# A hybrid decoder block: second and third gate matrices both by seven block products

## The reference, cut to what matters

```
h = rms_norm(x, norm_mix_pre)
a_h, a_b, a_c, c_a, c_g, s_u, s_v, g_a, g_c, g_s = split(h @ w_in)      # ten 1024-wide parts
y_a = a_b * conv3(a_c * a_h)
y_c = silu(layer_norm(conv31(c_a * sigmoid(c_g)) + b))
y_s = gelu(s_u) * (W_s @ layer_norm(gelu(s_v)) + b_s)
merged = sigmoid(g_a) * (y_a @ w_branch[0]) + sigmoid(g_c) * (y_c @ w_branch[1])
       + sigmoid(g_s) * (y_s @ w_branch[2])
x = x + rms_norm(merged @ w_out, norm_mix_post)          # then a squared-ReLU MLP, 1024 -> 4096 -> 1024
```

## Time and profile before

| | |
|---|---|
| time, median of 3 runs | 949.27 us (949.09 to 950.10) |
| the profiled execution's own time | 950.25 us |
| its span, first to last instruction | 948.5 us |
| mean granted TensorE clock | 0.998 |
| PE busy | 938.9 us (99%) |
| DVE busy | 738.4 us (78%) |
| ACT busy | 444.8 us (47%) |
| POOL busy | 110.0 us (12%) |
| DRAM traffic over the span | 241 GB/s |

### The profile page before, as it was taken

One profiled execution on the slowest core, in us unless ns is written; L12 is line 12 of the kernel. 1 busy time (PEld: TensorE's weight loads), 2 busy tenths in 40 slices (PEclk: granted clock), 3 DMA queues, 4 the chain that ended last, 5 costly groups with the idle time before them and its releaser, 6 DMA issues.

```text
span 948.5 us, 13659 instructions
## 1 busy us (share of the span) xinstructions
PE 938.9 (99%) x4967; PEld 811.5 (86%) x4967; DVE 738.4 (78%) x865; ACT 444.8 (47%) x548; POOL 110.0 (12%) x145
## 2 busy tenths in 40 slices
PE   8999999999999999999999999999999999999997
PEld 7888888888888888888889988899889989989985
DVE  5578978878878988886589575589875875786698
ACT  6533333333333322224368443377745745754774
POOL 1211101001100002222210000121001001100101
PEclk9999999999999999999999999999999999999999
DMA  8467779678776844444597674438586765858763
GB/s 308 152 208 245 233 216 271 187 233 247 196 226 213 218 133 133 133 133 134 149 262 237 217 221 135 178 137 242 155 259 128 236 176 148 232 135 242 197 203 111
DMA packets 45503, 185.36 MB, mean 195 GB/s; under 512 B 5305, under 2 KB 7745, under 8 KB 42177
## 3 DMA queue, kind: packets, MB, share of 16 engines
q1 hardware_dynamic: 32880, 115.52, 34.4%
q0 software_dynamic: 8432, 44.57, 24.2%
q10 hardware_dynamic: 4144, 24.65, 7.0%
HBM read 178.42 MB, written 49.81 MB: 241 GB/s over the span
## 4 chain that ended last, share of the span: by engine, by line
PE 97%; DVE 1%; DMA 1%; issue 0%; ACT 0%; ACTq 0%; DVEq 0%
PE ps L1944 25%; PE ps L1948 25%; PE ps L1946 25%; PE ps L2174 6%; PE ps L2176 6%; PE ps L2178 6%; PE ps L2139 1%; PE ps L2143 1%; PE ps L2141 1%; PE ps L2026 1%; DMA glu<-xt_in 1%; PE ps L2083 1%; PE ps L1989 0%; DVE wide L1782 0%; DVE wide L1799 0%
## 5 line engine op out<-in xcount | busy, mean ns | idle before, releaser
L853 ACT ACTIVATE w_hi<-raw 128x1024 fp32r<-128x1024 f32 (+1 forms) x140 | 146.0, 1052 | 233.7 <-DMA raw<-units_in 122.1
L1340 DVE TENSOR_TENSOR w_lo<-raw,w_hi 128x1024 fp32r<-128x1024 f32 (+1 forms) x141 | 172.0, 1226 | 72.0 <-ACT w_hi L853 68.8
L1429 DVE SCALAR_TENSOR_TENSOR conf<-glu,cols,conf (+1 forms) x240 | 186.8, 778 | 27.5 <-DVE conf L1429 26.4
L1944 PE MATMUL ps<-a_hi,w_hi 128*128 128x512 f32 x512 | 200.0, 391 | 0.0
L1948 PE MATMUL ps<-a_hi,w_lo 128*128 128x512 f32 x512 | 199.3, 389 | 0.0
L1946 PE MATMUL ps<-a_lo,w_hi 128*128 128x512 f32 x512 | 199.2, 389 | 0.0
L1948 PEld LDWEIGHTS ps<-a_hi,w_lo 128*128 128x128 f32 x512 | 96.1, 188 | 20.1
L1946 PEld LDWEIGHTS ps<-a_lo,w_hi 128*128 128x128 f32 x512 | 96.2, 188 | 19.7
L1944 PEld LDWEIGHTS ps<-a_hi,w_hi 128*128 128x128 f32 x512 | 96.1, 188 | 19.7
L1944 PE MATMUL ps<-w_hi,h_hi 128*128 128x512 f32 x220 | 85.8, 390 | 0.1
L1946 PE MATMUL ps<-w_lo,h_hi 128*128 128x512 f32 x220 | 85.6, 389 | 0.0
(11 more groups left out here) (225 smaller groups left out, 1785.8 us busy)
## 6 DMA issues: line engine op xcount, KB each, us to landing
raw<-units_in SPq DMA_DIRECT2D x123, 512.0 KB, 4.2
weight_sums<-units_in POOLq DMA_DIRECT2D x18, 1024.0 KB, 8.4
raw<-weight_sums SPq DMA_DIRECT2D x20, 512.0 KB, 4.3
raw_v<-units_in SPq DMA_DIRECT2D x18, 512.0 KB, 6.6
glu<-units_in SPq DMA_DIRECT2D x16, 512.0 KB, 8.2
glu<-units_in POOLq DMA_DIRECT2D x16, 512.0 KB, 5.5
raw_d<-units_in POOLq DMA_DIRECT2D x15, 512.0 KB, 6.7
glu<-weight_sums SPq DMA_DIRECT2D x9, 512.0 KB, 5.6
```

Of the source, the lines that this page charges most:

```text
L853: return nc.scalar.activation(dst, src, ACT.Copy, scale=scale)
L1340: return nc.vector.tensor_tensor(dst, src, hi, ALU.subtract)
L1429: nc.vector.scalar_tensor_tensor(out=conf[:, tile, :], in0=glu[:, tile, k:k + SEQ], scalar=cols[:, tile, COL_CONF + k:COL_CONF + k + 1], i ...
L1944: nc.tensor.matmul(ps[:, bank, :], left_hi, right_hi, start=first, stop=False, skip_group_check=on_top)
```

## The change

g_s is taken out of the pairs and done by seven block products as g_c is; the differences of x are made once and serve both matrices. The order becomes: w_branch[2] on y_s alone by eight channel units (`U_BS`, units 72 to 79), its result copied by ACT from PSUM into `bs_home`; then 28 gate units (`U_G`, 80 to 107): products 1, 2, 4 of g_s (80 to 85), 1, 2, 4 of g_c (86 to 91), 5, 3, 6, 7 of g_s (92 to 99), 5, 3, 6, 7 of g_c (100 to 107); then w_branch[1] (108 to 115). The layer norm of y_c now runs under units 72 to 79 and the first gate units. `statistic(0)` stands behind unit 75, `statistic(1)` behind unit 78. The sum of squares moves from POOL to DVE. POOL issues eight more DMAs of 1 MB for the block sums of the second matrix, two for each made product. DVE multiplies gate and branch of g_s in four blocks (`gate_s`) into `merged`. The split of y_c moves to between products 6 and 7 of g_c. The reload of x for the residual moves into the w_branch[1] stage, in two parts. Core of the diff:

```diff
-U_G = U_GATE + 4 * KT
-G_UNITS = 14
+U_BS = U_GATE + 2 * KT
+U_G = U_BS + KT
+G_UNITS = 28
 U_B = U_G + G_UNITS
...
-G_MADE = (5, 7, 6, 4)
+G_MADE = (5, 6, 4, 7)
 G_SUMS = MATRICES * MADE_UNITS
 G_FIRST = {5: (0, 0), 7: (1, 1), 6: (1, 1), 4: (1, 0)}
 G_SECOND = {5: (0, 1), 7: (0, 1)}
 G_SOURCE = {6: 5, 4: 6}
-G_ORDER = (1, 2, 4, 5, 3, 6, 7)
-G_BANK = {1: 0, 6: 0, 7: 0, 2: 4, 4: 6, 5: 2, 3: 2}
+G_ORDER = ([(m, product) for m in (GATE_S, GATE_C) for product in (1, 2, 4)] +
+           [(m, product) for m in (GATE_S, GATE_C) for product in (5, 3, 6, 7)])
+G_BANK = ({1: 0, 6: 0, 7: 0, 2: 2, 4: 4, 5: 2, 3: 2}, {1: 6, 6: 6, 7: 6, 2: 2, 4: 4, 5: 4, 3: 4})
 G_ON_TOP = (6, 7, 3)
...
-        g_home = nrm
-        g_of = {name: g_home[:, CH * n:CH * (n + 1), HALF_T * t:HALF_T * (t + 1)]
-                for name, (t, n) in {"22": (0, 0), "21": (0, 1), "11": (1, 1), "12": (1, 0)}.items()}
+        g_home = over("g_home_s", [P, KT, SEQ], "b_lo"), conf
+        bs_home = over("bs_home", [P, KT, SEQ], "b_hi")
+        def g_blocks(home):
+            return {name: home[:, CH * n:CH * (n + 1), HALF_T * t:HALF_T * (t + 1)]
+                    for name, (t, n) in {"22": (0, 0), "21": (0, 1), "11": (1, 1), "12": (1, 0)}.items()}
+        g_of = g_blocks(g_home[GATE_S]), g_blocks(g_home[GATE_C])
+        bs_of, merged_of = g_blocks(bs_home), g_blocks(merged)
...
-                    g_sum(G_MADE[(j - 1) // 2], (j - 1) % 2)
+                    g_sum(GATE_S, G_MADE[(j - 1) // 2], (j - 1) % 2)
...
-                    g_sum(G_MADE[3], 1)
+                    g_sum(GATE_S, 7, 1)
+                elif j == 3:
+                    g_sum(GATE_C, 5, 0)
+                elif j == 5:
+                    g_sum(GATE_C, 5, 1)
+                    g_sum(GATE_C, 6, 0)
+                else:
+                    g_sum(GATE_C, 6, 1)
...
-            for j in range(1, KT):
-                pool.wait_ge(squared, j + 1)
-                if j > 1:
-                    pool.wait_ge(sq_sum, j - 1)
-                nc.gpsimd.tensor_tensor(nrm[:, 0, :], nrm[:, 0, :], nrm[:, j, :],
-                                        ALU.add).then_inc(sq_sum, 1)
+            for n, (product, step) in enumerate(((4, 0), (4, 1), (7, 0), (7, 1))):
+                pool.wait_ge(unit_done, U_BS + 2 * n + 1)
+                g_sum(GATE_C, product, step)
             for m in range(KT // 2, MATRICES):
-                pool.wait_ge(unit_done, U_GATE + 2 * (KT + m) + 2)
+                pool.wait_ge(unit_done, U_G + 4 * (m - KT // 2) + 1)
                 second_block(m, 7)
...
+                act.wait_ge(silu, CH * (n + 1))
...
+            for j in range(KT):
+                u = Count(U_BS + j)
+                after(u)
+                nc.scalar.activation(bs_home[:, j, :], ps[:, j % 4, :], ACT.Copy)
+                split_hi(u.plus(RING))
+                if j == 2:
+                    act.wait_ge(chan_sum, KT)
+                    copy_hi(stat_hi[:, :], u_act[:, :]).then_inc(stat_hi_ready, 1)
+                elif j in (3, 4):
+                    for t in range(4 * (j - 3), 4 * (j - 2)):
+                        act.wait_ge(centred, t + 1)
+                        nc.scalar.activation(nrm[:, t, :], conf[:, t, :], ACT.Square).then_inc(squared, 1)
+                elif j == 5:
+                    act.wait_ge(sq_sum, KT - 1)
+                    act.wait_ge(stat_done, 1)
+                    copy_hi(stat_hi[:, :], nrm[:, 0, :]).then_inc(stat_hi_ready, 1)
+                elif j == 6:
+                    act.wait_ge(var_step, 2)
+                    nc.scalar.activation(y_s[:, :], y_s[:, :], ACT.Sqrt).then_inc(conf_rstd, 1)
+            tanh_of(range(0, 3))
+            g_behind(0)
+            tanh_of(range(3, 5))
+            load_xn(0)
+            g_behind(1)
+            tanh_of(range(5, KT))
+            load_xn(1)
+            g_set_hi("22-21", 1)
+            g_behind(2)
+            g_behind(3)
+            g_keep(GATE_S, 1, "22")
+            g_behind(4)
+            g_set_hi("21+12-11-22", 3)
+            g_behind(5)
+            g_keep(GATE_S, 4, "12")
...
+            def y_c_hi_of(tiles):
+                act.wait_ge(merged_ready, KT)
+                for t in tiles:
                     copy_hi(b_hi[:, t, :], nrm[:, t, :], 0.5).then_inc(y_c_hi, 1)
+            y_c_hi_of(range(CH))
+            g_behind(24)
+            y_c_hi_of(range(CH, KT))
+            g_behind(25)
+            g_gate(GATE_C, "21", 10)
+            g_behind(26)
+            g_behind(27)
+            g_gate(GATE_C, "11", 14)
+            g_gate(GATE_C, "12", 14)
...
+            def gate_s(n, name, tanh):
+                dve.wait_ge(g_tanh, tanh)
+                nc.vector.scalar_tensor_tensor(out=g_of[GATE_S][name], in0=g_of[GATE_S][name], scalar=1.0,
+                                               in1=bs_of[name], op0=ALU.add, op1=ALU.mult).then_inc(gated, 2)
+                dve.wait_ge(gated, KT + 2 * n + 2)
+                nc.vector.tensor_tensor(merged_of[name], merged_of[name], g_of[GATE_S][name],
+                                        ALU.add).then_inc(merged_ready, 2)
             for j in range(KT):
+                u = Count(U_BS + j)
                 after(u)
                 split_lo(u.plus(RING))
+                if j == 2:
+                    dve.wait_ge(stat_hi_ready, 1)
+                    lo(stat_lo[:, :], u_act[:, :], stat_hi[:, :]).then_inc(stat_lo_ready, 1)
+                elif j in (3, 4):
+                    for t in range(4 * (j - 3), 4 * (j - 2)):
                         dve.wait_ge(stat_done, 1)
                         nc.vector.tensor_tensor(conf[:, t, :], conf[:, t, :], ps[:, 4, :],
                                                 ALU.subtract).then_inc(centred, 1)
+                    for t in range(max(1, 4 * (j - 3)), 4 * (j - 2)):
+                        dve.wait_ge(squared, t + 1)
+                        if t > 1:
+                            dve.wait_ge(sq_sum, t - 1)
+                        nc.vector.tensor_tensor(nrm[:, 0, :], nrm[:, 0, :], nrm[:, t, :],
+                                                ALU.add).then_inc(sq_sum, 1)
+                elif j == 5:
+                    dve.wait_ge(stat_hi_ready, 2)
+                    lo(stat_lo[:, :], nrm[:, 0, :], stat_hi[:, :]).then_inc(stat_lo_ready, 1)
+                elif j == 6:
                     dve.wait_ge(stat_done, 2)
                     nc.vector.tensor_scalar(y_s[:, :], ps[:, 5, :], EPS, None, ALU.add).then_inc(var_step, 1)
                     dve.wait_ge(var_step, 1)
                     nc.vector.reciprocal(y_s[:, :], y_s[:, :]).then_inc(var_step, 1)
+                    for t in range(KT):
+                        dve.wait_ge(conf_rstd, 1)
+                        nc.vector.tensor_tensor(conf[:, t, :], conf[:, t, :], y_s[:, :],
+                                                ALU.mult).then_inc(scaled, 1)
+            def silu_of(tiles):
+                for t in tiles:
                     dve.wait_ge(silu_th, t + 1)
                     nc.vector.scalar_tensor_tensor(out=nrm[:, t, :], in0=conf[:, t, :], scalar=1.0,
+                                                   in1=nrm[:, t, :], op0=ALU.add, op1=ALU.mult).then_inc(silu, 1)
+            silu_of(range(0, 3))
+            g_behind(0)
+            silu_of(range(3, 5))
+            g_behind(1)
+            silu_of(range(5, KT))
+            dve.wait_ge(xn_loaded[0], 16)
+            g_less("22-21", "22", "21")
+            g_behind(2)
+            g_set_lo("22-21", 1)
+            g_behind(3)
+            g_join(GATE_S, 2, "22", 1)
             dve.wait_ge(xn_loaded[1], 16)
+            dve.wait_ge(g_diff, 1)
             g_minus("21-22-11", "22-21", "11")
             dve.wait_ge(g_diff, 2)
             g_minus("21+12-11-22", "21-22-11", "12")
+            g_less("11-21", "11", "21")
+            g_behind(4)
             g_set_lo("21+12-11-22", 2)
+            g_behind(5)
...
+            g_done(24)
+            g_join(GATE_C, 6, "21", 10, 0)
+            g_behind(24)
+            y_c_lo_of(range(CH))
+            g_done(25)
+            g_join(GATE_C, 6, "21", 10, 1)
+            g_behind(25)
+            y_c_lo_of(range(CH, KT))
             for h in range(2):
+                g_done(26 + h)
+                g_join(GATE_C, 7, "11", 10, h)
+                g_join(GATE_C, 7, "12", 10, h)
+                g_behind(26 + h)
...
+            pe.wait_ge(y_s_lo, KT)
             for j in range(KT):
-                u = Count(U_GATE + 2 * KT + 2 * j)
-                channel_unit(u, a_hi, a_lo, 2 * (j % 2))
-                if j == 2:
+                channel_unit(Count(U_BS + j), c_hi, c_lo, j % 4)
+                if j == 3:
                     statistic(0)
-                pe.wait_ge(y_s_lo, KT)
-                channel_unit(u.plus(1), c_hi, c_lo, 2 * (j % 2) + 1)
-                if j == 4:
+                elif j == 6:
                     statistic(1)
...
             pe.wait_ge(y_c_lo, KT)
+            pe.wait_ge(g_joined, 8)
```

(20 more changed lines are left out.)

316 lines of the change are left out of this document (134 added, 182 removed).

## The result

The changed kernel takes **977.04 us** (970.91 to 978.52) against 949.18 (948.88 to 950.10): ratio 1.0285, interval 1.0245 to 1.0325. It is slower, by 27.9 us. The profiled execution is the shortest of the four, 970.91, with a mean granted clock of 0.992; the other three had 0.985 to 0.988.

A forecast was written before the change was run, and what follows sets the result against it. PE was taken to bound the kernel, busy 99% with almost no wait. Waits of 5.1 + 12.2 + 2.4 + 3.1 = 22.8, less 3.7 saved, gave +19.1: 969.3 for a profiled execution, 968.4 us as median, range 956 to 977.

The forecast's parts named there:

- The saving: On PE: g_s falls from 43.5 to 40.3 us and an old 0.48 wait leaves its place, together -3.7 us.
- First wait: At `statistic(0)`: PE waits for `stat_lo` behind the split of unit 78 and its load; 5.1 us, bounds 4.0 to 6.2.
- From `statistic(0)` to X: Up to the start of `statistic(1)`, called X: DVE's mean subtraction and squares fit under units 76 to 78; nothing, bound 0.5.
- POOL's extra DMAs: Eight extra DMAs on POOL's queue, waiting on one another; costed at nothing.
- Second wait: From `statistic(1)` to unit 86: splits queued behind the layer norm's tail and reloaded x; 12.2 us, bounds 9.9 to 14.2.
- Unit 88: Third wait: seven DVE pieces, 8.1 us, between `w_lo` of 86 and 88, against two PE units, 5.76; 2.4 us.
- the clock rival: Matmuls behind PE's gaps run at 1.2 GHz instead of 2.4; 2 to 4 us more, 970.4 to 972.4; chance 17%.
- Units 107 and 108: Last waits: a join behind a late split and four `y_c_lo`, 2.4, then 0.7; together 3.1 us, 5.3 at most.
- the prediction's own signs of being wrong: No wait at the first statistic, a `statistic(1)`-to-86 chain well off 35 us, or new waits between units 92 and 106.
- The reload of x for the residual: In two parts, later, but covered by w_out's stage; costed at nothing, bound 2 if not covered.
- From one execution to the median, "0.98 below": The old kernel's median lay 0.98 below its profiled execution, so 969.3 for an execution became 968.4 as median.
- Long loads: Rival: landings at the upper ends everywhere, waits of 28.1 less 3.7, so 973.7 us; chance 11%.

The follow-up runs named there:

- norm_first: Changed kernel with the layer norm's steps ahead of the splits of units 78 to 81 on ACT and DVE; 966.46 us, ratio 1.0194.
- stat_apart: Changed kernel with the two statistic tiles over y_a and duo, so load 82 no longer waits for the second statistic; 967.04 us, ratio 1.0184.
- plain_first: Changed kernel with the splits of units 86 to 89 ahead of the differences of x on ACT and DVE; 969.70 us, ratio 1.0217.
- y_c_fill: Changed kernel with DVE's first four y_c_lo ahead of the split of unit 108, product 7's join ahead of the other four; 973.31 us, ratio 1.0234.
- all_turned: all_quiet with the splits of units 90 and 91 moved ahead of differences of x and their splits; 953.97 us, ratio 1.0052.
- stat_first: Changed kernel with the split of the first statistic ahead of the split of unit 78 on ACT and DVE; 974.62 us, ratio 1.0271.
- after: The changed kernel itself, first set, against the kernel before; 977.04 us, ratio 1.0285.
- sums_late: Changed kernel with POOL's last four block sums of the third gate matrix issued only when the second branch is done; 981.07 us, ratio 1.0334.
- all_fixed: Changed kernel with norm_first, stat_apart, y_c_fill and plain_first's order together, single splits spread between the last tanh and silu tiles; 959.85 us, ratio 1.0100.
- all_quiet: all_fixed with POOL's four later block-sum DMAs issued behind units 92, 96, 100 and 104 instead of 80, 84, 88 and 92; 956.48 us, ratio 1.0064.
- the second set: The changed kernel run once more, nothing edited, in another set; 972.61 us, ratio 1.0244.

## Why the prediction was right, and where it was not

**The direction and the places were right.** Forecast was slower, by waits at the first statistic, at units 83, 85, 86, 88 and 107, each behind a named instruction. All six are in the trace, with the releasers named, and the runs that moved those instructions took the waits away: at the first statistic (`norm_first`), at 83 (`stat_apart`), at 88 and half of 86 (`plain_first`), at 107 (`y_c_fill`).

**The size: 968.4 was forecast, 977.04 came**, 0.04 above the end of the range. In the profiled execution the sum of 969.3 meets 970.91, but only because two errors cancel: the waits sum to 18.6 where 22.8 were taken, and the half pace of 6.0 was not in the sum. By its terms, the waits as brackets of PE's timeline:

- *The saving*, 3.7: borne out by the account. Even in `all_turned` it is not enough: the waits and the half pace that are left, 5.6 + 3.0, exceed it.
- *First wait*, 5.1 (4.0 to 6.2): 3.56 (3.7 in the account), below the lower bound, because load 78 took 3.1; the middle between 3.2 and 5.4 was wrong. The wait was there, but taking it away bought nothing by itself (`stat_first`): see the next.
- *From `statistic(0)` to X, "cost nothing, bound 0.5"*: **this step failed.** It counted DVE's work and left out that the work stands behind the split of unit 79. That load took 6.4, beside POOL's copy, and pins X: in after `stat_lo` ends at 451.87, 0.3 before PE asks, so no wait shows there, but without the first wait 6.21 stand at X (`stat_first`). The prediction put POOL's extra DMAs at nothing here and asked of load 78 alone whether the copy would make it long; load 78 took 3.1 although the copy was issued 0.9 after it, and the next load took the company.
- *Second wait*, 12.2 (9.9 to 14.2): 9.5 (2.70 + 0.56 + 6.23; 10.0 in the account). The chain from X to the split of 86 is 33.5 (452.19 to 485.64) against 35.4: load 82 took 3.5 where 5.5 was taken. The parts of the chain are as forecast, with the reload of x at 7.6 where 6.7 was taken.
- *Unit 88*, 2.4: 1.58. PE came 1.5 later, at half pace behind 86, so the clock ate into this wait, as the clock rival said; without it the wait would have been some 3.1, as `g_minus` waited for the second half of x (10.0 us).
- *Units 107 and 108*, 3.1: 2.24, and nothing at 108, where PE comes 1.4 us later at half pace. A small wait of 0.63 at unit 98 was not foreseen; a new wait between 92 and 106 was one of the prediction's own signs of being wrong. The reload of x for the residual cost nothing, as forecast (411.4 against 411.6 us from w_branch[1] to the end).
- *The clock rival* (2 to 4 on top, 17%): right as a mechanism. Three stretches at half pace lost 1.6, 1.5 and 1.4 us; of these the first lies under the pin of load 79 and the second in the wait at 88. For the warm-up matmuls, from which the prediction took the half rate, the profile of before shows a granted clock of 1.00 (1.3 to 5.3 us), so there only the pitch of 0.45 speaks for it; behind the waits of after the granted clock shows it. The Trainium skill (TensorE: Matmul & The Clock Gate, "The HAM clock gate") says that idleness brings the half rate back; the trace agrees, 0.43 against 0.227 behind a wait of 3.56.
- *From one execution to the median, "0.98 below"*: **this step failed too.** Executions of the kernel before agree within 1.0 to 2.5 us in a set; those of after spread over 7.6, since PE here stands behind loads whose landings scatter. Load 82 took 3.5 in one execution and 8.6 in another (`y_c_fill`, 977.96 us), load 79 6.3 to 8.7 beside POOL's copy. `sums_late` speaks for the copies beside these loads as the cause: it has the longest waits of all, but no copy beside loads 78 to 83, and its executions agree within 0.8 us. Long loads, 973.7, with the clock's 2 to 4 on top come to 976 to 978, where the median lies; I gave the first 11%. The Trainium skill (DMA: Bandwidth & Descriptors, "Issuing engines are not separate DMA queues") says that DMAs of all issuing engines run on the same 16 DMA engines and interleave. `all_fixed` against `all_quiet` agrees: 10.7 and 4.6 for the same two loads.

**Open.** The three executions at 976.5 to 978.5 left no trace (nor did a fifth, at 978.36, which is not in the median). That late landings and the clock behind them made them long is argued from the execution of `y_c_fill` at 977.96, not shown for them; why the second set ran 4.4 lower is not known either.

## What to carry to other kernels

Before a matrix is made cheaper on a bound engine, walk the queues of the other engines through the new order: a split that waits for its load holds back whatever stands behind it, and a saving of 3.7 us does not pay for one such place. When one wait is removed, name the next link on the same queue before counting the gain; here it took six edits before the next link was an engine's own work. And a kernel whose bound engine stands behind loads can have a scatter that one profiled execution does not show, so where other transfers run beside those loads its forecast needs the longer landings in the middle of the range, not at its end.
